# A convolution stage: low parts of the weights on GpSimd instead of VectorE, and eight taps per chunk on TensorE instead of ten

## What is computed

```python
CONV_WIDTH = 31
def dwconv(x, w):
    return lax.conv_general_dilated(x, w[:, None, :], window_strides=(1,), padding='SAME',
                                    dimension_numbers=('NWC', 'WIO', 'NWC'),
                                    feature_group_count=x.shape[-1])

def conformer_conv(u, rows, w_pw1, b_pw1, w_dw, b_dw, ln_g, ln_b, w_pw2, b_pw2):
    a = u @ w_pw1 + b_pw1
    a = a[..., :CONV_DIM] * jax.nn.sigmoid(a[..., CONV_DIM:])
    bsz, s, ch = a.shape
    if rows is None:
        a = dwconv(a, w_dw)
    else:
        a = dwconv(a.reshape(bsz * rows, GRID_W, ch), w_dw).reshape(bsz, s, ch)
    a = jax.nn.silu(layer_norm(a + b_dw, ln_g, ln_b))
    return a @ w_pw2 + b_pw2
```

## Time and profile before

| | us |
|---|---|
| median of 3 runs | 3007.77 (3007.25 to 3009.14) |
| the profiled execution | 3006.21 |
| its span | 3004.40 |
| TensorE busy | 2949.9 (98%) |
| VectorE busy | 2129.7 (71%) |
| ScalarE busy | 1192.7 (40%) |
| GpSimd busy | 193.5 (6%) |

### The profile page before, as it was taken

The page is one execution under the profiler, slowest core; times in us unless marked ns, Lnnn a source line. Parts: engine busy times, 40 slices in busy tenths (PEclk is TensorE's granted clock), DMA queues, the critical chain, the costliest instruction groups (busy, mean ns, idle before and its releaser), DMA issues.

```text
span 3004.4 us, 40234 instructions
## 1 busy us (share of the span) xinstructions
PE 2949.9 (98%) x14353; PEld 2420.3 (81%) x14353; DVE 2129.7 (71%) x3282; ACT 1192.7 (40%) x1803; POOL 193.5 (6%) x163
## 2 busy tenths in 40 slices
PE   7999999999999999999999999999999999999998
PEld 5888678888887789977888888788888888876787
DVE  6973688877786788699898876566754632756875
ACT  3223524332143664556441323443244422423443
POOL 2300000000001000000040210000000000002120
PEclk9999999999999999999999999999999999999999
DMA  7672065666633156311266552672366622452554
GB/s 276 200 245 92 21 197 174 215 202 240 205 102 112 57 182 222 129 57 43 99 208 212 175 183 76 213 248 100 102 219 215 215 91 92 150 188 95 199 186 144
DMA packets 125230, 479.26 MB, mean 160 GB/s; under 512 B 13752, under 2 KB 13752, under 8 KB 122768
## 3 DMA queue, kind: packets, MB, share of 16 engines
q1 hardware_dynamic: 119232, 443.60, 44.5%
q0 software_dynamic: 5840, 33.51, 3.1%
HBM read 459.23 MB, written 17.83 MB: 159 GB/s over the span
## 4 chain that ended last, share of the span: by engine, by line
PE 79%; issue 10%; DVE 6%; ACT 2%; DMA 1%; SPq 0%; POOL 0%; DVEq 0%; ACTq 0%; POOLq 0%
PE bank L798 21%; PE bank L800 21%; PE bank L799 21%; PE bank L811 4%; PE bank L812 2%; PE bank L1727 2%; PE bank L1100 1%; DVE x_res L2667 1%; DVE w_lo L2551 1%; PE bank L810 1%; DMA ada_first<-in_ada 1%; DVE x_res L2673 1%; PE bank L1206 1%; ACT w_hi L1795 1%; DMA ml_v<-v_spill 0%
## 5 line engine op out<-in xcount | busy, mean ns | idle before, releaser
L2551 DVE TENSOR_TENSOR w_lo<-w_raw,w_hi 128x1024 fp32r<-128x1024 f32 x617 | 754.7, 1231 | 498.1 <-ACT w_hi L1795 489.1
L1795 ACT ACTIVATE w_hi<-w_raw 128x1024 fp32r<-128x1024 f32 x620 | 649.5, 1055 | 755.6 <-PE bank L800 626.4
L798 PE MATMUL bank<-h_hi,w_hi 128*128 128x512 f32 (+1 forms) x1432 | 524.5, 366 | 7.3 <-DVE h_lo L2640 5.2
L799 PE MATMUL bank<-h_lo,w_hi 128*128 128x512 f32 (+1 forms) x1432 | 518.9, 362 | 0.0
L800 PE MATMUL bank<-h_hi,w_lo 128*128 128x512 f32 (+1 forms) x1432 | 518.8, 362 | 0.0
L798 PEld LDWEIGHTS bank<-h_hi,w_hi 128*128 128x128 f32 x1432 | 270.4, 189 | 54.9 <-issue 9.7
L799 PEld LDWEIGHTS bank<-h_lo,w_hi 128*128 128x128 f32 x1432 | 270.4, 189 | 43.7 <-issue 1.2
L800 PEld LDWEIGHTS bank<-h_hi,w_lo 128*128 128x128 f32 x1432 | 270.3, 189 | 41.6
L798 PE MATMUL bank<-w_hi,xm_hi 128*128 128x512 f32 x512 | 201.0, 393 | 0.1
L800 PE MATMUL bank<-w_hi,xm_lo 128*128 128x512 f32 x512 | 199.4, 389 | 0.0
L799 PE MATMUL bank<-w_lo,xm_hi 128*128 128x512 f32 x512 | 199.3, 389 | 0.0
(11 more groups left out here) (473 smaller groups left out, 5667.3 us busy)
## 6 DMA issues: line engine op xcount, KB each, us to landing
w_raw<-in_weights SPq DMA_DIRECT2D x620, 512.0 KB, 4.2
ada_ring_f<-in_ada SPq DMA_DIRECT2D x56, 512.0 KB, 3.4
ada_ring_g<-in_ada SPq DMA_DIRECT2D x44, 512.0 KB, 3.4
ada_ring_b<-in_ada SPq DMA_DIRECT2D x38, 512.0 KB, 4.2
ada_ring_a<-in_ada SPq DMA_DIRECT2D x32, 512.0 KB, 3.4
ada_first<-in_ada SPq DMA_DIRECT2D x16, 512.0 KB, 15.3
v_spill<-ml_v POOLq DMA_DIRECT2D x4, 1024.0 KB, 6.9
o_spill<-ml_o_grp POOLq DMA_DIRECT2D x4, 1024.0 KB, 4.6
```

What stands on the lines that cost most here:

```text
L798: mm(out, lhs[0], rhs[0], start=start, stop=False)
L799: mm(out, lhs[0], rhs[1], start=False, stop=False)
L1795: return nc.scalar.activation(out, in_, func, **kw)
L2551: V.tensor_tensor(WLO[:, slot, :], RAW[:, slot, :], WHI[:, slot, :].bitcast(F32), SUB)\
```

## The change

`PE_TAPS` of chunks 1 to 6 goes from 10 to 8, so VectorE does 21 taps there instead of 19. The low parts of 14 weight tiles (pw1's tiles 5 to 15 and pw2's tiles 0 to 2, each made three tiles ahead) are made by GpSimd, in one loop behind the clearing of `conv_in`. VectorE keeps the two before them and those after them, and gets a wait ahead of its next one.

```diff
-PE_TAPS = [14] + [10] * 6 + [15]
+PE_TAPS = [14] + [8] * 6 + [15]
@@ gpsimd
             own(pool.memset(CIN[:, :, :], 0.0))
 
+            def weight_low(n):
+
+                pool.wait_ge(S("w_hi_done"), n + 1)
+                pool.tensor_tensor(WLO[:, n % SLOTS, :], RAW[:, n % SLOTS, :], WHI[:, n % SLOTS, :].bitcast(F32), SUB)\
+                    .then_inc(S("w_lo_done"), 1)
+
+            first = FIRST["pw1"] + LOOKAHEAD
+            pool.wait_ge(S("w_lo_done"), first + 2)
+            for t in range(2, 16):
+                weight_low(first + t)
+
@@ vector, per chunk
                 conv_input(p)
                 acc0, acc1 = CACC[:, 2 * (p % 2), :], CACC[:, 2 * (p % 2) + 1, :]
 
-                if p:
-                    lo_ahead("pw1", t - 1, t - 1)
-                if 0 < p < DC - 1:
-                    lo_ahead("pw1", t, t)
                 conv_lo(p)
...
                 own(V.tensor_tensor(acc0, acc0, acc1, ADD))
-                if p == DC - 1:
-                    lo_ahead("pw1", t, t)
                 dve.wait_ge(S("conv_pe_done"), p + 1)
@@ vector, layer norm of the convolution
                 if s == 8:
+                    dve.wait_ge(S("w_lo_done"), FIRST["pw2"] + LOOKAHEAD)
                     lo_ahead("pw2", 0, 0)
```

## The result

| | before | after |
|---|---|---|
| median of 6 runs each, us | 3007.51 (3006.17 to 3009.14) | 3019.9 (3018.38 to 3022.17) |
| ratio to before | 1 | 1.0043 [1.0033, 1.0053] |
| span of the profiled execution, us | 3004.4 | 3016.7 |
| TensorE, VectorE, GpSimd busy, us | 2949.9, 2129.7, 193.5 | 2947.6, 2135.2, 276.7 |
| mean granted clock of TensorE | 0.997 | 0.995 |

The changed kernel is slower by 12.4 us. The forecast was slower by 29.5: the sign is right and the size is not. In the changed kernel's lines the taps are L3283, the sum of the two accumulators L3289, `conv_z` L3291, the low part of the input L3265, GpSimd's low parts L725.

What follows compares the result with a forecast made beforehand. TensorE (98% of the span) bounds the kernel, nearly level with VectorE in the convolution, where VectorE becomes the bound alone; -2.5 + 30.0 + 2.0 = +29.5 us on 3007.77 gives 3037.2 us, range 3032 to 3041.

Steps and rivals of the forecast that it cites:

- VectorE's own pace: Convolution chunks 1 to 6: two more taps +1.32, low parts removed -1.34, so 18.34 us a chunk instead of 18.36.
- ScalarE's conversion: Convolution chunks: with the low parts gone, ScalarE's conversion of the conv input leaves VectorE 0.97 us idle.
- the pair's 2.36 us: VectorE's two low parts in a convolution chunk take 2.36 us; removing them was claimed to save only 1.34 us.
- The size of a hold: Convolution taps: VectorE stands still 2.14 us for each GpSimd low part running beside them; bounds zero and 2.14.
- How many collide: Chunks 0 to 6: both GpSimd low parts of each chunk fall into VectorE's taps, 14 x 2.14 = 30.0 us.
- the MLP rows: MLP stage before the change: GpSimd's instruction came at 1524.37; VectorE's next took 2.31 instead of 1.22 us.
- When GpSimd asks: Later chunks, C being TensorE's taps start: first high part about C + 6, second C + 13.2, within taps until C + 16.
- The clock: Before chunk 7's taps TensorE stands about 8.5 us, then runs some 4 us at half speed: +2.0 us, bounds 0 and 11.
- the 14.25 worked out: Chunk 7's own part, bound by TensorE's fifteen taps: 14.25 us instead of 14.46, without any clock loss.
- -2.5: Convolution stage without collisions or clock loss: its end comes at 1400.0 against 1402.5, a gain of 2.5 us.
- Rival 2: Convolution chunks: seven low parts collide, through a late second high part or gapless taps keeping GpSimd out; 3022.3 us, 12%.
- the 74%: Chance given to the main forecast of 3037.2 us, with all 14 GpSimd low parts holding VectorE's convolution taps.

## Why the prediction was right in sign and wrong in size

**VectorE's own pace: right.** 18.34 us a chunk was worked out, and 20.35 - 2.01 is 18.34. That VectorE becomes the bound alone and TensorE waits, that ScalarE's conversion lies open by 0.97 and that only 1.34 of the pair's 2.36 us comes off were right too. The half with the taps alone gave +1.34 for the +1.32.

**The size of a hold: nearly right.** 2.14 us was taken from the kernel's start. The held sum shows 2.01; held taps, where there are some, 2.14 (2.88 - 0.74).

**How many collide: wrong, and this is the step that failed.** All 14 were charged; 7 are. The failed inference is the sentence on the MLP rows: "There VectorE ran without a gap, and GpSimd got in at the next boundary all the same, which is the situation of the taps." It is not. In the MLP a low part was followed by another kind of instruction; in the row a tap is followed by a tap like it. The two like instructions of the earlier trace rows were no case of it either, since VectorE read out an accumulator between them and the first had already been held:

```profile
40.43 0.08 DVE L2566 DVE_READ_ACCUMULATOR ada_junk_a<-ada_first,c_rows 128x1 f32 x1
```

GpSimd stood through eleven boundaries between taps and got in at the first other one. There two things come together: the sum is another operation, and it waits for the last tap, which leaves 0.1 us (1294.27 to 1294.38). The experiments show that inside the row either is enough, a wait ahead of a like tap or a one-column instruction without a gap. Getting in there costs VectorE one hold, on the sum, and the second low part falls into the 2.7 us in which VectorE has no second SBUF input. 7 x 2.01 = 14.1 us instead of 30.0.

**When GpSimd asks: wrong, without effect.** The second high part was put at C + 13.2, behind the next pw1 tile. It is ready 1.5 us after the first. Either time lies in the row, and at either the first low part was still standing.

**The clock: right in kind, 0.4 us low.** A loss of 2.0 was expected behind a gap, after 8.5 us of standing; it was 2.4, behind 5.4 us. The gap is shorter because the chunks are. (With the wait in the row TensorE stood 6.39 us there, and chunk 7 took 16.10 us against the 14.25 worked out, which is 1.9.)

**The sum again.** -2.5 + 14.1 + 2.4 = +14.0 us, against 13.9 in the stage. Rival 2 in its second branch, "the gapless taps keep GpSimd out until that stretch", is what happened, at 3022.3 for 3019.9. That rival had 12% for both its branches, though no row of before showed a first request in the middle of a row of like instructions: the 74% rested on a case that had not been seen.

The Trainium skill ("SBUF — State Buffer", "Who interferes with whom") says that the instruction issued first has the shared port for its whole length and the other blocks. What was held here agrees, each time for one whole GpSimd instruction (2.01 to 2.14 us). But it speaks of pairs. Read as the prediction read it, GpSimd should have got in behind the tap during which it asked, and the trace shows it standing for eight microseconds.

## What to carry to other kernels

Moving work to GpSimd beside a VectorE that is the bound costs one hold for each GpSimd instruction that gets in ahead of an instruction with two SBUF inputs (2.0 to 2.1 us for 128x1024 fp32 here, 0.9 for 128x512). What decides is where it gets in, so look at the instruction that follows a run of like ones, and put one-input work (a PSUM read) there. Don't break such a run with a wait or a small instruction while GpSimd is waiting: seven gaps of 0.2 us cost 15 us here. And take an engine's slack in the stage, not its share of the kernel: VectorE was 71% busy over the kernel and 99% in this stage, so taking low parts from it and giving it taps back left its pace where it was (18.34 for 18.36 us) before the first collision.

## What was not expected of the hardware

- A GpSimd instruction with SBUF inputs that is ready while VectorE runs a row of like instructions with two SBUF inputs can stand for the whole rest of the row: from 1286.4 to 1294.3 us in chunk 1, in all of the chunks 0 to 6.
- A one-column instruction in the row lets it in, with one SBUF input (the tap behind it took 2.82 us) or with two, then even of the taps' own operation (it took 2.35 us itself); so does a wait that leaves a gap of 0.2 us (row 18.29 us instead of 13.99).
- After a tap has been held, a later request gets in between two ordinary taps (asked at 1294.90, held tap from 1294.97). After a one-column instruction has been held, it does not, for nine taps. What decides who gets the port is open; no run here tells the two remaining readings apart.
- GpSimd's one-column clearings, which only write, ran beside the taps (44 in 1.52 us from 1293.43, beside taps of 0.74 us) and were neither held nor held a tap.
- Instructions of VectorE that read one input from PSUM and one from SBUF were never held (`conv_z` 0.686 to 0.689 us in all eight chunks of the changed kernel, in seven of them while GpSimd's second low part was at work).
